# Two layers of a hybrid mixer with 64 experts: the down weights in one 8 KB piece per partition, the hidden units dealt out at a stride of two

## The reference

```
scores = sigmoid(h @ router_w);  idx = top_k(scores + router_bias, 8)
gate   = scores[idx] / sum(scores[idx]) * 2.5
for each expert e of 64:   rows xb = the tokens that chose e
    out = (silu(xb @ w_gate[e]) * (xb @ w_up[e])) @ w_down[e]
    result[token] += gate * out
```

## Time and profile before

| | |
|---|---|
| median of 3 runs | 2814.97 us (2814.79 to 2819.05) |
| the profiled execution | 2812.39 us, span 2810.7 us |
| granted TensorE clock, mean | 0.948 of 2.4 GHz |
| TensorE busy in the span | 2448.0 us, 87% |
| VectorE busy | 1266.5 us, 45% |
| ScalarE and GpSimd busy | 23% and 22% |
| DMA, hardware queue (SyncE's) | 162,950 packets, 520.48 MB, 49.8% of 16 engines |
| DMA, software queue (GpSimd's) | 24,832 packets, 51.97 MB, 8.0% |
| all packets | 187,920, of which 148,870 under 8 KB |

### The profile page before, as it was taken

The page is one execution under the profiler, slowest core; times in us unless marked ns, Lnnn a source line. Parts: engine busy times, 40 slices in busy tenths (PEclk is TensorE's granted clock), DMA queues, the critical chain, the costliest instruction groups (busy, mean ns, idle before and its releaser), DMA issues.

```text
span 2810.7 us, 45706 instructions
## 1 busy us (share of the span) xinstructions
PE 2448.0 (87%) x15116; PEld 1632.2 (58%) x15117; DVE 1266.5 (45%) x2832; ACT 643.9 (23%) x1146; POOL 610.6 (22%) x640
## 2 busy tenths in 40 slices
PE   5999888886789999999996798888877999999994
PEld 2347788885645555555553345787865555555552
DVE  4433487875333333333332553467853333333333
ACT  2116343231111111111110114523321111111111
POOL 0000354550002222222221000245320122222221
PEclk9999899997899999999998799999989999999998
DMA  6643100001539999999996251200017899999993
GB/s 259 244 175 76 19 2 1 1 1 35 195 136 319 367 352 349 344 343 341 364 336 192 99 201 60 49 1 1 1 43 276 314 365 374 376 354 361 364 367 115
DMA packets 187920, 574.26 MB, mean 204 GB/s; under 512 B 55742, under 2 KB 99078, under 8 KB 148870
## 3 DMA queue, kind: packets, MB, share of 16 engines
q1 hardware_dynamic: 162950, 520.48, 49.8%
q0 software_dynamic: 24832, 51.97, 8.0%
HBM read 554.89 MB, written 53.15 MB: 216 GB/s over the span
## 4 chain that ended last, share of the span: by engine, by line
PE 58%; DVE 15%; DMA 14%; issue 5%; ACT 4%; POOLq 2%; DVEq 2%; ACTq 1%; POOL 0%; SPq 0%
PE ps L1732 53%; DMA featT<-ffn_rows,idx_in 8%; PE ps L1736 5%; DVE R L1098 3%; DMA R<-ffn_rows,idx_in 3%; ACT R L832 2%; DVE featT L1098 2%; DVE ring L1098 1%; POOLq L744 1%; DVE R L1372 1%; DMA R<-in_exp_up 1%; ACT L832 1%; DVEq L1095 1%; DVE R L1101 1%; DMA R<-ffn_sum_even 1%
## 5 line engine op out<-in xcount | busy, mean ns | idle before, releaser
L1732 PE MATMUL ps<-R 128*64 128x256 f32 (+6 forms) x9040 | 1391.4, 379 | 68.9 <-DVEq L1377 19.3
L1732 PEld LDWEIGHTS ps<-R 128*64 128x64 f32 (+2 forms) x9040 | 850.1, 162 | 477.2 <-issue 250.5
L832 ACT ACTIVATE R<-ps 128x256 f32<-128x256 f32 (+3 forms) x395 | 175.5, 444 | 1047.7 <-PE ps L1732 993.7
L1098 DVE TENSOR_TENSOR R<-R,ps 128x256 f32<-128x256 f32 (+2 forms) x250 | 143.7, 575 | 439.8 <-ACT R L832 368.5
L1732 PE MATMUL ps<-featT,ring 128*128 128x512 f32 (+1 forms) x768 | 312.5, 563 | 0.3 <-issue 0.3
L1732 PE MATMUL ps<-ring,R 128*128 128x128 f32 (+2 forms) x1200 | 242.4, 334 | 16.3 <-DVE ring L1098 7.8
L1732 PEld LDWEIGHTS ps<-featT,ring 128*128 128x128 f32 x768 | 147.2, 196 | 161.8 <-issue 156.9
L1732 PEld LDWEIGHTS ps<-ring,R 128*128 128x128 f32 x1200 | 191.9, 196 | 49.1 <-issue 28.7
L1101 DVE TENSOR_SCALAR R<-ps,idx_out 128x512 f32<-128x512 f32 x128 | 96.1, 751 | 270.9 <-PE ps L1732 270.9
L1107 DVE COPY R<-ps 128x512 f32<-128x512 f32 (+2 forms) x280 | 153.8, 549 | 129.9 <-PE ps L1736 96.4
L669 POOL TENSOR_TENSOR R<-ring,lev 128x512 f32<-128x512 f32 x56 | 73.0, 1303 | 618.5 <-DVEq L1334 307.3
(11 more groups left out here) (201 smaller groups left out, 1974.3 us busy)
## 6 DMA issues: line engine op xcount, KB each, us to landing
R<-in_exp_gate SPq DMA_DIRECT2D x128, 1024.0 KB
R<-in_exp_up SPq DMA_DIRECT2D x128, 1024.0 KB
R<-in_exp_down SPq DMA_DIRECT2D x128, 1024.0 KB
R<-in_w_mod SPq DMA_DIRECT2D x48, 1024.0 KB, 7.4
ring<-in_w_in SPq DMA_DIRECT2D x30, 1024.0 KB, 5.3
ring<-in_w_out SPq DMA_DIRECT2D x8, 1024.0 KB, 8.0
ffn_sum_odd<-zero SPq DMA_DIRECT2D x6, 512.0 KB, 11.1
ffn_rows<-X SPq DMA_DIRECT2D x6, 512.0 KB, 5.4
```

The costliest lines, as they stand in the source:

```text
L832: do(C.activation(out_, in_, func, **kw), name)
L1098: do(V.tensor_tensor(out_, a, b, op), name)
L1732: return MM(out_, lhsT, rhs, start=start, stop=stop)
```

## The change

The down weights are read with rows 2p and 2p + 1 of the matrix in partition p, which is one contiguous piece of 8 KB in device memory, as gate and up already are. So that the second operand fits, the hidden units are split into even and odd instead of first and second half: gate and up products read their weights' columns at a stride of two. The same two edits are made in the path for experts with more than 128 rows. Buffers, semaphores, the order of issue and the number of instructions and DMAs are as before.

```
-                down_w = A["exp_down"][L1].rearrange("o e (k p) n -> p (o e) k n", p=P)
+                down_w = A["exp_down"][L1].rearrange("o e (p k) n -> p (o e) (k n)", p=P)
...
-                    sp.dma_start(wdn[s][:, :, :], down_w[:, one].rearrange("p e k n -> p (e k) n")).then_inc(S[f"wd{s}"], 16)
+                    sp.dma_start(wdn[s][:, :, :].rearrange("p k n -> p (k n)"), down_w[:, one].rearrange("p e f -> p (e f)")).then_inc(S[f"wd{s}"], 16)
...
-                                sp.dma_start(wdn[0][:, :, :], down_w[:, one].rearrange("p e k n -> p (e k) n")).then_inc(S["ov_w"], 16)
+                                sp.dma_start(wdn[0][:, :, :].rearrange("p k n -> p (k n)"), down_w[:, one].rearrange("p e f -> p (e f)")).then_inc(S["ov_w"], 16)
...
-                            ins = mm(ps[:, 2 + b, q * P:q * P + n], wgu[s][:, q // 2, k, tk(q % 2)], xgT[b][:, k, 0:n], k == 0, k == KT - 1)
+                            ins = mm(ps[:, 2 + b, q * P:q * P + n], wgu[s][:, q // 2, k, q % 2:ED:2], xgT[b][:, k, 0:n], k == 0, k == KT - 1)
...
-                                     xgT[b][:, k, u * HD:(u + 1) * HD], wgu[s][:, :, k, tk(half)], k == 0, k == KT - 1)
+                                     xgT[b][:, k, u * HD:(u + 1) * HD], wgu[s][:, :, k, half:ED:2], k == 0, k == KT - 1)
```

## The result

The changed kernel takes 2826.02 us (median of 14 runs, 2820.86 to 2830.48), the kernel before 2814.23 us beside it (14 runs): ratio 1.0048, 95% interval 1.0038 to 1.0058, 11.8 us slower. The profiled execution is one of 2829.26 us, its span 2827.5 us. The forecast was 2,809 us. The time lies in the range, but on the other side of no change.

A forecast was written before the change was run, and what follows sets the result against it. In the expert stages TensorE (96% and 95% busy) and the DMA engines (99% and 98%) were both taken as near their limit. Terms -9 + 3 + 0 = -6 us gave 2,809 us, range 2,799 to 2,840.

The forecast's parts named there:

- the moving columns: Gate and up products: columns at a stride of two cost between nothing and a factor of two; nothing taken.
- the pieces: Down weights in 8 KB pieces: 9 us gained on loads, 3 us lost by gathers behind larger packets.
- rival D: Gate and up products: the stride costs, 5.8 us per cent of slower streaming, 3,390 us at a factor of two; chance 0.05.
- The bound of 1.7 ns a column: Most the stride could cost, from `h_products` steps of 64 columns: 0.11 us / 64.
- Down loads: Expert loops' down loads: 8 KB packets save about 16 ns per 4 KB pair, 16 us at most; 9 us taken.
- The sign named in the prediction: Hardware queue: packets under 8 KB should fall by 16,384.
- gathers: Expert loops: gathers land later behind larger packets, 29 us at full price; most returned, so 3 us taken.
- rival C: Expert loops: gathers late behind 8 KB packets, nothing returned, 2,844 us; with half returned, 2,829; chance 0.25.
- Rival B: Expert loops: DMA saving hidden in a long queue or eaten by later gathers, -4 to +5 us, 2,815; chance 0.27.
- fast steps of 8.43 and 11.87 us: Expert loops: TensorE's fixed time per narrow and wide expert; where these bound, the down loads gain nothing.
- the overflow path: Path for experts with more than 128 rows: same two edits, no cost or gain expected.
- a gate and up pass takes more than 3.67 us: Gate and up pass of 32 products: should stay 3.67 us; a longer one would show the forecast wrong.

The follow-up runs named there:

- experiment 6: Changed kernel with gate and up columns read at a stride of four over two neighbouring blocks of the contraction: 3357.14 us (one run).
- experiment 1: Kernel before with only the gate and up columns at a stride of two, down weights still in 4 KB pieces: 2821.3 us, ratio 1.0044.
- experiment 2: Kernel before with only the down weights in 8 KB pieces, columns contiguous: 2815.62 us, ratio 1.0012.
- experiment 7: Kernel before with gate and up weights in 4 KB pieces instead of 8 KB, gathered rows stored to match: 2803.08 us, ratio 0.9974.
- experiment 5: Changed kernel with the second half of the columns taking its contraction blocks in the order 4 to 7, 0 to 3: 2827.74 us, ratio 1.0069.
- experiment 8: Kernel before with gate and up weights in 2 KB pieces, gathered rows stored to match: 2838.74 us, ratio 1.0098.

## Why the prediction was wrong

The forecast was -6 us and the change cost 11.8, so 18 us were missed, and two terms of the sum share them about equally: the moving columns, priced at 0, cost 9.7 us, and the pieces, priced at -9 + 3 = -6, cost 4.1. With the stride priced rightly the sum would still have been some 8 to 10 us short.

*The first step that failed* is the one on the moving columns: "Of the two ends I take nothing, since the strided row shows no sign of a cost beside its contiguous neighbour." The row compared was one of products of 64 columns that go every 0.11 us at a stride of two and without one; as the text itself said, something else set their pace. Such a row bounds a cost, and doesn't price it. In the gate and up pass, whose time follows its columns (experiment 6 doubles it), the stride adds 0.18 us to 3.67, 5%. By the prediction's own rule for its rival D (162 passes, 5.8 us for each per cent) that is 28 us of TensorE's time; 24.4 us show in the group's busy time and 9.7 us arrive at the end. D, given a chance of 0.05, is one half of what happened, in a mild form. The bound of 1.7 ns a column turned out to be near the price at a stride of four, 1.81 ns.

*Why 28 us came out as 10.* In the first layer 93 passes are 93 x 0.18 = 17 us; the stride alone lengthened that stage by 4.9 us, with 11.0 us more of busy time (642.70 us in its window above) and 5 us less of idle. The gate and up group itself is busy 16.2 us more there; the down product, 602 ns in the mean before and 595 now, and the turns give 4 us back, which fits fewer stretches at the lower clock, since TensorE waits less. The window of the kernel before, from its first pass to its last, is

```profile
841.00:1497.00 656.00, 631.73 (x4275) 372.27 (x4276) 222.57 (x555) 103.91 (x187) 153.60 (x122) 0.99 0.97 340
```

The second layer has 69 passes, 12 us, and its length did not change: 572.7 and 573.0 us, the latter with 70 passes. In six of the table's eight runs with pieces of 4 KB or more it is 571 to 574 us (the others 568.9 and 575.1); DMA moves 357 GB/s there in the kernel before, the changed one (357 and 358 in its two profiles) and experiments 1, 2 and 7 alike, at a share of 0.97 to 1.00. So that stage seems to follow its transfers and the gathers in them, and a longer pass goes into waits. That the slack was there, the prediction had said ("TensorE has 23 us (624 - 601) and 31 us (574 - 543) of idle to give back").

*Down loads, 9 us of gain taken.* All packets fell by 16,384 (187,920 to 171,536). The sign named in the prediction, those under 8 KB, fell by twice that, 148,870 to 116,102: each load lost 256 pieces of 4 KB and got 128 of 8 KB. The price of a packet held as well as it could be read: three microseconds of the second layer's fill gave

```profile
DMA packets 176, 1.25 MB, mean 415 GB/s; under 512 B 24, under 2 KB 24, under 8 KB 24
...
q1 hardware_dynamic: 176, 1.25, 99.6%
```

(2159 to 2162 us), 0.996 x 16 x 3 / 152 = 315 ns for one of 8 KB, against 312. A window with down packets alone could not be told apart, since all weights have one size now. What arrived with the pieces alone is 6.7 us less waiting for weights: the mechanism is there, and the size of 9 us was somewhat too large.

*The second step that failed: gathers, 3 us of loss taken.* Mis-sized: "I think most of this is returned, and take 3 us." The waits grew by 9.1 us with the pieces alone, a third of the full 29, and the slower work after them, which the forecast left out of this term though its rival C priced it, came on top. The return to DMA that the text relied on exists, but it did not make the term small. So the DMA part of the sum is -6.7 + 9.1 = +2.4 us in the profiles, +4.1 us in the medians (interval 0.8 to 5.9), and not -6. Rival B had this part right, between hidden and eaten by the gathers. C's mechanism, gathers later behind larger packets, is shown by the times to landing of experiments 5, 7 and 8 (8.6, 7.6 and 7.2 us); the gather waits, from 9.3 us at 2 KB to 54.2 us at 8 KB, go the same way, with a part of the fall at 2 KB due to TensorE's own waits for weights. In the changed kernel it does not show as longer waits at all, 41.1 and 45.5 us against 45.1, since the longer passes cover it: 34.3 us, with the stride alone, is what it must be held against.

*What held:* fast steps of 8.43 and 11.87 us as what mainly sets the first layer (its 35 narrow steps and 28 wide ones from the first pass to the last come to 627 of 656.9 us), no change from the overflow path (both kernels issue 384 loads of expert weights, those of the loops, so it did not run), and the prediction's test "a gate and up pass takes more than 3.67 us", which found the first fault.

*Open:* Why two floats apart costs 5% where the line rule gives nothing; experiment 5 only excludes that the two streams' reads of the same block do it. Whether the gathers are held up packet by packet in turn, or by what is already inside an engine, was not separated either.

## What to carry to other kernels

Price a strided moving operand from a product that is bound by its columns; one whose pace something else sets showed no cost at a stride of two. Where gathers of a software queue share the engines with a bulk stream, the best packet may be neither the largest nor the smallest: here 8 KB made the gathers late, 2 KB starved the weights, and 4 KB for all weights was 0.3 to 0.4% faster than the kernel before and some 0.8% faster than the changed one. And a part of a change that has a cover must be judged with the other part undone: the gather waits of the changed kernel looked unharmed until the stride was taken out.

## What the runs showed of the hardware

- fp32 moving columns at strides of one, two and four elements: 3.67, 3.85 and 7.42 us for 32 instructions of 256 columns, two at a time on the array. The 5% at two is there with the second stream on another block too.
- Eight 64x64 products with the identity (16 instructions) in place of two turns cost 0.70 against 0.42 us, and the next pass began 0.48 to 0.70 us late.
- Pieces of 8, 4 and 2 KB for the gate and up weights, same bytes: 2815.62 (with the down weights at 8 KB too), 2803.08 and 2838.74 us, an optimum in the middle, while gather waits fall from 54.2 to 9.3 us and weight waits rise from 5.6 to 66.4.
- A gather takes a median of 8.6, 7.6 and 7.2 us from issue to landing behind gate and up pieces of 8, 4 and 2 KB on DMA engines that are busy for 0.95 to 0.99 of the first layer's stage, and 4.6 us behind 8 KB pieces where they are busy for 0.70 of it.
